# Solved 32x32 blocks of a delta rule: returned in four transfers to a compact tile, then placed by ScalarE and GpSimd

## What is computed

```
def _gated_delta_rule(q, k, v, beta, g):
    """S_t = exp(g_t) S_{t-1} (I - beta_t k_t k_t^T) + beta_t k_t v_t^T ; o_t = S_t^T q_t"""
    ...
    kb = k * beta[..., None]
    a_mat = jnp.where(strict, jnp.einsum("bhnid,bhnjd->bhnij", kb, k) * decay, 0.0)
    a_mat = a_mat + jnp.eye(c, dtype=q.dtype)
    rhs = jnp.concatenate([v * beta[..., None], kb * jnp.exp(g)[..., None]], axis=-1)
    sol = lax.linalg.triangular_solve(a_mat, rhs, left_side=True, lower=True,
                                      unit_diagonal=True)
    u, w = sol[..., :dv], sol[..., dv:]
    ...
    def step(state, inp):
        q_i, k_i, u_i, w_i, attn_i, gl_i = inp
        v_new = u_i - jnp.einsum("bhcd,bhde->bhce", w_i, state)
        ...
```

## Time and profile before

| | us |
|---|---|
| median of three runs | 3819.69 |
| lowest, highest | 3818.0, 3825.82 |
| span of the profiled execution | 3823.0 |
| TensorE busy in it | 3710.3 (97%) |
| VectorE busy | 2048.9 (54%) |
| ScalarE busy | 1089.4 (28%) |
| GpSimd busy | 69.4 (2%) |

### The profile page before, as it was taken

One profiled execution on the slowest core, in us unless ns is written; L12 is line 12 of the kernel. 1 busy time (PEld: TensorE's weight loads), 2 busy tenths in 40 slices (PEclk: granted clock), 3 DMA queues, 4 the chain that ended last, 5 costly groups with the idle time before them and its releaser, 6 DMA issues.

```text
span 3823.0 us, 43694 instructions
## 1 busy us (share of the span) xinstructions
PE 3710.3 (97%) x17964; PEld 3007.1 (79%) x17964; DVE 2048.9 (54%) x2527; ACT 1089.4 (28%) x1199; POOL 69.4 (2%) x80
## 2 busy tenths in 40 slices
PE   9999999989999999999999999999999998999998
PEld 8878888856778887888876678888888875778887
DVE  6564434563654445443766764434443766665443
ACT  3342222242432222222343222222222343322221
POOL 0000000000000000000110000000000102000000
PEclk9999999999999999999999999999999999999999
DMA  4212222110222222222412222222222413122221
GB/s 150 100 66 99 96 94 99 62 39 24 88 95 99 96 92 94 92 94 105 141 37 94 80 83 93 99 95 95 95 96 92 147 60 100 67 77 88 99 94 72
DMA packets 67766, 343.04 MB, mean 90 GB/s; under 512 B 23748, under 2 KB 23748, under 8 KB 32048
## 3 DMA queue, kind: packets, MB, share of 16 engines
q1 hardware_dynamic: 61872, 303.25, 22.4%
q0 software_dynamic: 5760, 37.86, 2.6%
HBM read 324.31 MB, written 16.78 MB: 89 GB/s over the span
## 4 chain that ended last, share of the span: by engine, by line
PE 88%; DVE 8%; ACT 2%; issue 1%; DMA 0%; SPq 0%; DVEq 0%; ACTq 0%
PE ACC L1003 26%; PE ACC L1004 25%; PE ACC L1005 25%; PE ACC L1669 1%; PE ACC L1497 1%; PE MIX L1497 1%; DVE WL L2340 1%; DVE PT L3172 0%; DVE PT L3170 0%; PE MIX L1724 0%; PE ACC L1411 0%; PE MIX L1462 0%; PE ACC L1010 0%; PE MIX L1423 0%; PE ACC L1657 0%
## 5 line engine op out<-in xcount | busy, mean ns | idle before, releaser
L1003 PE MATMUL ACC<-HH,WH 128*128 128x512 f32 (+1 forms) x3322 | 1305.6, 393 | 18.9 <-DVE X L2439 5.3
L1004 PE MATMUL ACC<-HL,WH 128*128 128x512 f32 (+1 forms) x3322 | 1290.4, 388 | 0.0
L1005 PE MATMUL ACC<-HH,WL 128*128 128x512 f32 (+1 forms) x3322 | 1290.4, 388 | 0.0
L2340 DVE TENSOR_TENSOR WL<-RAW,WH 128x2048 fp32r<-128x2048 f32 x291 | 667.4, 2293 | 445.7 <-ACT WH L1836 445.2
L1003 PEld LDWEIGHTS ACC<-HH,WH 128*128 128x128 f32 x3322 | 625.7, 188 | 165.0 <-issue 17.7
L1004 PEld LDWEIGHTS ACC<-HL,WH 128*128 128x128 f32 x3322 | 625.7, 188 | 130.3 <-issue 5.0
L1005 PEld LDWEIGHTS ACC<-HH,WL 128*128 128x128 f32 x3322 | 625.7, 188 | 128.5
L1836 ACT ACTIVATE WH<-RAW 128x2048 fp32r<-128x2048 f32 x291 | 554.7, 1907 | 599.3 <-PE ACC L1005 591.0
L2449 DVE TENSOR_TENSOR SG<-ACC,RS 128x512 f32<-128x512 f32 x132 | 91.3, 692 | 626.8 <-PE ACC L1005 626.6
L1005 PE MATMUL ACC<-HIDH,WL 128*128 128x512 f32 x1056 | 411.3, 389 | 0.0
L1004 PE MATMUL ACC<-HIDL,WH 128*128 128x512 f32 x1056 | 411.3, 389 | 0.0
(11 more groups left out here) (529 smaller groups left out, 2907.2 us busy)
## 6 DMA issues: line engine op xcount, KB each, us to landing
RAW<-wall SPq DMA_DIRECT2D x260, 1024.0 KB, 4.7
RAW<-wall SPq DMA_DIRECT2D x24, 768.0 KB, 4.1
KR<-spectra POOLq DMA_DIRECT2D x4, 2048.0 KB, 9.0
x_kept<-X POOLq DMA_DIRECT2D x2, 2048.0 KB, 6.8
FWK<-mats POOLq DMA_DIRECT2D x4, 1024.0 KB, 5.5
spectra<-SQ POOLq DMA_DIRECT2D x8, 512.0 KB, 3.0
spectra<-T POOLq DMA_DIRECT2D x8, 512.0 KB, 3.4
X<-x_kept POOLq DMA_DIRECT2D x2, 2048.0 KB, 14.5
```

Of the source, the lines that this page charges most:

```text
L1003: pe.matmul(out_ap, wh, hh, start=first, stop=False)
L1004: pe.matmul(out_ap, wh, hl, start=False, stop=False)
L1005: return pe.matmul(out_ap, wl, hh, start=False, stop=last)
L2340: v.tensor_tensor(WL[n % 2][:], RAW[n % 2][:], WH[n % 2][:], ALU.subtract).then_inc(w_lo, 1)
```

## The change

The two writes are cut by direction so that `blocks_out` is ordered by block row b first. Four reads, one per block row, bring everything into CB, a compact tile of 2 directions x 16 matrices x 32 columns on each of the 128 partitions. CB lies where BX lay, CT where the scratch BT lay. VectorE turns CB into CT, two transposes of 256 columns per pair. The first level reads CB and CT. ScalarE (`place_turned`) copies the blocks onto the diagonal of XIT, GpSimd onto that of XI, eight copies of 32 partitions x 256 columns each per pair; the second level waits for both. GpSimd zeroes all of XIT and, after the last spectrum is issued, XI[:, 1]. One semaphore now counts all four reads.

```diff
@@ sync
                     sp.wait_ge(blocks_solved, L + 1)
-                    sp.dma_start(blocks_out, BX[:]).then_inc(solved_sent, 16)
-                    sp.wait_ge(solved_sent, 16 * (L + 1))
-                    sp.wait_ge(dn_zero, 3 * L + 3)
-                    for p in range(2):
-                        for b in range(4):
-                            rows = slice(32 * b, 32 * b + 32)
-                            for d, dst in ((0, XI), (1, XIT)):
-                                src = blocks_out.rearrange("(d b p m) r x -> d b p r m x", d=2, b=4, p=2)[d, b, p]
-                                sp.dma_start(dst[rows, d, 8 * p:8 * p + 8, rows], src).then_inc(solved_landed[p], 16)
+                    for d in range(2):
+                        sp.dma_start(blocks_out.rearrange("(b d q) r x -> d b q (r x)", b=4, d=2)[d],
+                                     BX[64 * d:64 * d + 64].rearrange("p r x -> p (r x)")).then_inc(solved_sent, 16)
+                    sp.wait_ge(solved_sent, 32 * (L + 1))
+                    for b in range(4):
+                        src = blocks_out.rearrange("(b m) r x -> b r m x", b=4)[b]
+                        sp.dma_start(CB[32 * b:32 * b + 32].rearrange("p d m x -> p (d m) x"), src).then_inc(solved_landed, 16)
@@ gpsimd
                         if n == 4:
                             pool.wait_ge(kf_sp, 4 * l + 2)
-                            pool.memset(XIT[:, 1], 0.0).then_inc(dn_zero, 1)
+                            pool.memset(XIT[:], 0.0).then_inc(dn_laid, 1)
                         pool.wait_ge(kf_ev, 8 * l + n + 1)
                         pool.dma_start(spectra[o, :, fc, 2 * i:2 * i + 2], (SQ, T)[i][:]).then_inc(kf_out[i], 16)
+                    pool.wait_ge(kf_sp, 4 * l + 4)
+                    pool.memset(XI[:, 1], 0.0).then_inc(dn_laid, 1)
                     pool.wait_ge(kf_fd, 8 * l + 8)
                     for i in range(2):
                         pool.wait_ge(kf_out[i], 64 * (l + 1))
                     pool.dma_start(KR[0][:], spectra[0]).then_inc(kf_back[0], 16)
+                    pool.wait_ge(dn_laid, 6 * l + 4)
+                    for p in range(2):
+                        pool.wait_ge(dn_xt, 2 * l + p + 1)
+                        m = slice(8 * p, 8 * p + 8)
+                        for b in range(4):
+                            rows = slice(32 * b, 32 * b + 32)
+                            pool.tensor_copy(XI[rows, 0, m, rows], CB[rows, 0, m, :])
+                            k = pool.tensor_copy(XI[rows, 1, m, rows], CT[rows, 1, m, :])
+                        k.then_inc(dn_laid, 1)
@@ tensor, left
                     if lev == 0:
-                        pe.wait_ge(dn_xt, 4 * L + h + 1)
+                        pe.wait_ge(dn_xt, 2 * L + p + 1)
...
                         pe.wait_ge(dn_tc, 12 * L + 6 * p + a + 3)
+                        pe.wait_ge(solved_placed, 2 * L + p + 1)
+                        pe.wait_ge(dn_laid, 6 * L + p + 5)
                     for c in range(TC):
                         for d in range(2):
                             for near, far in joined(d, lev):
-                                mm = pe.matmul(ACC[far, 2 * a + d, columns(c, near)], DT[near, h, d, c, far], XI[near, d, TC * h + c, near],
-                                               start=True, stop=True)
+                                x = solved(d, 0)[near, d, TC * h + c, :] if lev == 0 else XI[near, d, TC * h + c, near]
+                                mm = pe.matmul(ACC[far, 2 * a + d, columns(c, near)], DT[near, h, d, c, far], x, start=True, stop=True)
@@ scalar
+                def place_turned(p):
+                    act.wait_ge(dn_xt, 2 * L + p + 1)
+                    act.wait_ge(dn_laid, 6 * L + 3)
+                    m = slice(8 * p, 8 * p + 8)
+                    for b in range(4):
+                        rows = slice(32 * b, 32 * b + 32)
+                        act.activation(XIT[rows, 0, m, rows], CT[rows, 0, m, :], ACT.Copy)
+                        k = act.activation(XIT[rows, 1, m, rows], CB[rows, 1, m, :], ACT.Copy)
+                    k.then_inc(solved_placed, 1)
...
                 copy_left(0, 0, 0)
                 copy_left(0, 1, 0)
+                place_turned(0)
                 grown_keys(0, 1)
...
                 copy_values(0, 1)
+                place_turned(1)
                 grown_keys(1, 0)
@@ vector
                 def turn_blocks(p):
-                    v.wait_ge(solved_landed[p], 128 * (L + 1))
+                    v.wait_ge(solved_landed, 64 * (L + 1))
                     v.wait_ge(kf_sp, 4 * L + 4)
-                    for h in (2 * p, 2 * p + 1):
-                        m = slice(TC * h, TC * h + TC)
-                        v.transpose(XIT[:, 0, m].rearrange("p c n -> p (c n)"), XI[:, 0, m].rearrange("p c n -> p (c n)"))
-                        v.transpose(XI[:, 1, m].rearrange("p c n -> p (c n)"), XIT[:, 1, m].rearrange("p c n -> p (c n)")).then_inc(dn_xt, 1)
+                    m = slice(8 * p, 8 * p + 8)
+                    for d in range(2):
+                        t = v.transpose(CT[:, d, m, :].rearrange("p c n -> p (c n)"), CB[:, d, m, :].rearrange("p c n -> p (c n)"))
+                    t.then_inc(dn_xt, 1)
```

More of the change, by code:

```diff
@@ L671, in build @@
         dn_at = sem("dn_at")
-        dn_zero = sem("dn_zero")
+        dn_laid = sem("dn_laid")
         blocks_sent = sem("blocks_sent")
@@ L676, in build @@
         solved_sent = sem("solved_sent")
-        solved_landed = [sem(f"solved_landed{i}") for i in range(2)]
+        solved_landed = sem("solved_landed")
+        solved_placed = sem("solved_placed")
         dn_xt = sem("dn_xt")
@@ L831, in build @@
         BX = put("BX", [P, 32, 32])
+        CB = place("CB", [P, 2, 4 * TC, 32], at=put.at[0] - 4 * 1024)
+        CT = place("CT", [P, 2, 4 * TC, 32], at=put.at[0])
         put = arena(put.at[0] + 4 * 1024)
@@ L950, in _ @@
                     pool.memset(BX[:], 0.0)
-                    pool.memset(XI[:, 0], 0.0).then_inc(dn_zero, 1)
-                    pool.wait_ge(dn_zero, 3 * l + 1)
-                    pool.memset(BX[:].rearrange("p r x -> p (r x)")[:, 0:1024:33], 1.0).then_inc(dn_zero, 1)
+                    pool.memset(XI[:, 0], 0.0).then_inc(dn_laid, 1)
+                    pool.wait_ge(dn_laid, 6 * l + 1)
+                    pool.memset(BX[:].rearrange("p r x -> p (r x)")[:, 0:1024:33], 1.0).then_inc(dn_laid, 1)
                     for h in range(4):
@@ L1361, in columns, with solved @@
                     return slice(c * P + rows.start, c * P + rows.stop)
+                def solved(d, turned):
+                    return CB if d == turned else CT
                 def left(p, a, lev):
@@ L1387, in right @@
                                 for near, far in joined(d, lev):
-                                    mm = pe.matmul(ACC[far, 2 * a + d, columns(c, near)], XIT[far, d, TC * h + c, far], YS[far, a, d, c, near],
+                                    xt = solved(d, 1)[far, d, TC * h + c, :] if lev == 0 else XIT[far, d, TC * h + c, far]
+                                    mm = pe.matmul(ACC[far, 2 * a + d, columns(c, near)], xt, YS[far, a, d, c, near],
                                                    start=True, stop=True)
@@ L1399, in right_turned @@
                             for near, far in joined(d, lev):
-                                mm = pe.matmul(ACC[near, 2 * a + d, columns(c, far)], YS[far, a, d, c, near], XIT[far, d, TC * h + c, far],
+                                xt = solved(d, 1)[far, d, TC * h + c, :] if lev == 0 else XIT[far, d, TC * h + c, far]
+                                mm = pe.matmul(ACC[near, 2 * a + d, columns(c, far)], YS[far, a, d, c, near], xt,
                                                start=True, stop=True)
@@ L2974, in solve_blocks @@
                     v.wait_ge(blocks_landed, 32 * (L + 1))
-                    v.wait_ge(dn_zero, 3 * L + 2)
+                    v.wait_ge(dn_laid, 6 * L + 2)
                     step(v.tensor_copy(BA[0:64], BG[0:64].rearrange("p r x -> p x r")))
@@ L3000, in keep_right @@
                     v.wait_ge(dn_t, 12 * L + 6 * p + a + 1)
+                    v.wait_ge(dn_laid, 6 * L + 4)
                     h = 2 * p + a
```

## The result

The changed kernel takes 3848.19 us (median of four runs, 3842.84 to 3850.55) against 3819.39 of the kernel before beside it: a ratio of 1.0068, 95% interval 1.0053 to 1.0082, or 28.8 us more. The forecast was slower, 3837, in a range of 3818 to 3842; the sign is right and the time lies above the range. All ratios here leave out executions far outside the others, of which there are two: one of `one_write` (10377 us) and one of the kernel before beside it (4403 us).

A forecast was written before the change was run, and what follows sets the result against it. TensorE was taken as the bound (88% of the chain), with the blocks' return hidden under its dummies. First levels late by 6.1 and 6.5 us plus 4.4 of clock made 17.0 on 3819.7, so 3837 us, range 3818 to 3842.

The forecast's parts named there:

- The return is hidden with 0.9 us to spare: Kernel before: the solved blocks' turns end at 2058.05, under the dummy matmuls, 0.9 us before the first level at 2058.95.
- Four shares for the write: Write of the solved blocks: its outermost loop of 4 spreads it over 4 engines, 32 packets each, 3.8 us more.
- The write lands at 2053.4: Write of the solved blocks, delayed by spectrum writes on the same engines: lands at 2053.4, between 2052.7 and 2054.5.
- The reads in 3.7 us: Four reads back of the solved blocks: 4096 packets pass in 3.7 us, after 0.9 us from issue to first packet.
- The change does not move that.: GpSimd's KR load: still issued at 2055.5, as the added memset ends 2 us before the wait for the spectra.
- Turns: VectorE's turns before the first level: four of 512 columns become two of 256, 0.75 us for both (0.6 to 1.4).
- The clock: TensorE after a 6 us pause: next dummies and small matmuls at the lower clock, 2.2 us per layer (0 to 4).
- What moved onto the other engines: Copies on ScalarE (0.39 us each) and GpSimd (0.3 to 1.0), turns on VectorE: nothing added, 4.4 us at ScalarE's far end.
- Hidden: Rival: the blocks' return stays hidden under the dummies by 2 us; 3819.5 us, range 3816 to 3824; chance 0.25.
- Copies: Rival: GpSimd copies over 1.1 us delay the second level; at 2 us, 8.7 us per layer, 3837; chance 0.05.
- One layer or a tail: Rival: reads caught by KR's load in one layer, or a short tail in both; +6 to +9 us, 3827; chance 0.10.
- faster: Rival: whole kernel faster by over 0.2%, needing 8 us, with no mechanism seen; chance 0.05.

The follow-up runs named there:

- one_write: The changed kernel with the write of the solved blocks as one transfer of 128 rows again and eight reads instead of four; 3821.73 us against 3822.97, ratio 0.9994.
- before_k20: The kernel before with 20 dummy matmuls instead of 28 ahead of the first level, all else as it was; 3820.55 us against 3822.85, ratio 0.9994.
- the three loops: Three kernels from `one_write`, with gaps in `blocks_out` making the write's DRAM side a loop of 8, 4 or 2; 3841.18, 3840.9 and 3850.26 us against 3822.29.
- kr_later: The changed kernel with the KR load held until the four reads have landed; 3834.21 us against 3822.97, ratio 1.0028.
- loop8: `one_write` with a gap in `blocks_out` after every 16 blocks, so the write is a loop of 8 over 16 rows; 3841.18 us against 3822.29, one execution.
- write_alone: The kernel before with only the two writes put in, its sixteen reads following the new block order; 3846.46 us against 3822.97, ratio 1.0059.
- eight_writes: The changed kernel with its write cut into eight transfers of 16 neighbouring rows, same layout and four reads; 3826.12 us against 3822.97, ratio 0.9997.
- reads_first_k14: `one_write` with 14 dummies instead of 28 and the last two spectrum writes held until the reads have landed; 3817.46 us against 3823.74, ratio 0.9987.
- loop4: `one_write` with a gap in `blocks_out` after every 32 blocks, so the write is a loop of 4 over 32 rows; 3840.9 us against 3822.29, one execution.
- loop2: `one_write` with one gap in the middle of `blocks_out`, so the write is a loop of 2 over 64 rows; 3850.26 us against 3822.29, one execution.

## Why the prediction was right or wrong

**The return is hidden with 0.9 us to spare.** Right in what matters, and loose in a detail. With the write undone the level starts at the end of the dummies. But the level of the first head waits for the first two turns only, and those end at 2056.87 (the second starts at 2056.20 and takes 0.67), so it had 2.1 us; `before_k20` shows it, where that level starts 6.3 us after the first dummy. Nothing in the sum hung on it.

**Four shares for the write.** Right, as far as the count of packets in flight tells. It was argued from form; the three loops (6.9, 3.4 and 1.65 in flight for 8, 4 and 2) and the 4.0 of the changed kernel now show it. Which engines carry them the trace doesn't tell.

**The write lands at 2053.4.** Wrong, and this is the step where the forecast first failed: it landed 4.0 us later, at 2057.4. I priced 32 packets on an engine at the 0.16 us of a packet in the kernel before and added 0.7 us for the spectra. The write of the changed kernel in two stretches, SP's queue over 2047.4 to 2051.4, and then both queues over 2051.4 to 2057.0:

```profile
q1 hardware_dynamic: 51, 0.20, 24.9%
```

```profile
q0 software_dynamic: 267, 0.98, 50.9%
q1 hardware_dynamic: 84, 0.32, 14.5%
```

In the first 4.0 us four packets are in flight throughout (24.9% of 16 is 4.0), but only 51 pass, where 100 at 0.16 us would have fitted: 0.249 x 64 us / 51 = 0.31 us for each. So when the spectra come, 84 packets are left in place of some 30. These are at 0.155 us again (0.145 x 89.6 / 84), but only 2.3 are in flight, with 8.1 of the spectra's beside them (50.9% of 16). The slow packets cost 49 x 0.16 / 4 = 2.0 us. The sharing cost 5.6 - 84 x 0.16 / 4 = 2.2 us, of which I had 0.7. Together they are 3.5 of the 4.0 us, and 0.4 is the later start of the stage (the first issue at 2045.72 in place of 2045.36). The range for this term, to 2054.5, had no room for either: the duration of a packet was taken as a constant of its size.

**The reads in 3.7 us.** Not tested as such in the changed kernel, since the last one is caught. In `kr_later` they land 4.5 us after their first issue, where 0.9 + 3.7 were predicted. Three of the four reads of the changed kernel landed by 2061.1; only the last waited until 2067.99.

**"The change does not move that."** Wrong for KR's issue, and this is the term of the sum that failed: the level waits for the load's end, and the load came 3.9 us late. I looked at what GpSimd does ahead of it, and the added memset indeed ended 5.6 us before the wait did. But that wait is for the spectra, and the slow write was still under way beside them: the last two took 7.1 and 7.3 us from issue to landing in place of 3.2 and 3.8, and the load was issued at 2059.38, 3.9 us later than before. They were slow at their start as well as at their end. GpSimd's queue in a stretch of 1 us, the kernel before over 2051.5 to 2052.5 and the changed one over 2051.9 to 2052.9, each 1.3 us after the issue of the first of the two:

```profile
q0 software_dynamic: 97, 0.40, 96.4%
```

```profile
q0 software_dynamic: 5, 0.02, 16.8%
```

I had allowed 0.5 us for the engines' backlog, and at the wrong place. The catch itself was right: the last read lands with the load, at 2067.99 and 2067.88, the load 8.5 us after its issue (8.3 predicted). So the release is late by 3.7 us (2067.99 against 2064.3), nearly all of it because the load is. `loop8` shows the same catch with the load on time: late by 6.5 and 6.0 us, where 6.1 and 6.5 were predicted.

**Turns.** 0.77 us for two, 0.75 predicted. The level is late by 9.5 and 9.0 us where the sum had 6.1 and 6.5: 5.9 us too little over both layers.

**The clock.** The sign and the place were right, the size was too large. From the level to the keys the changed kernel takes 13.1 and 14.0 us where it took 12.0 and 12.5, so 2.7 us over both layers where I had 4.4. In the first layer's chain the ten dummies cost 1.3 us more and not 2.1 (3.75 for 2.43), and the level's small matmuls 0.4 and not 0.1. The 0.105 us that the forecast adds to a pass is near what the trace of the kernel before has: the dummies' passes start 0.213 us apart from 2052.24 to 2054.80, at a grant of 0.50, and 0.111 us apart from 2055.17 to 2058.74, at 1.00. But the grant was 0.50 only until 2072.66, and the ten dummies, from 2069.92, ran 3.75 us. Another 2.8 us stand in the convolution of layer 1. Its windows, the kernel before and then the changed one:

```profile
2149.44:2213.25 63.81, 55.57 (x245) 42.84 (x246) 52.15 (x43) 7.71 (x8) 0.00 (x0) 0.95 0.14 50
```

```profile
2160.33:2226.98 66.65, 58.42 (x245) 44.75 (x246) 52.12 (x43) 7.71 (x8) 0.00 (x0) 0.90 0.13 48
```

The same 245 instructions take 2.8 us more at a grant of 0.90 in place of 0.95. These can't be put down to the change. `one_write`, which loses nothing, has the same 0.90 in its second layer, and `write_alone`, which has nearly the whole loss, has 0.95 in both. The second layer of `one_write`, then the first of `write_alone`:

```profile
3327.67:3394.33 66.66, 58.42 (x245) 44.80 (x246) 52.14 (x43) 7.71 (x8) 0.00 (x0) 0.90 0.13 48
```

```profile
2156.38:2220.21 63.83, 55.59 (x245) 42.79 (x246) 52.14 (x43) 7.71 (x8) 0.00 (x0) 0.95 0.13 50
```

So what is left for the clock, in this trace, are the 2.7 us behind the two levels. They are a balance: 3.3 us more up to the second level, and 0.6 less from there to the keys, where VectorE has fewer columns to turn.

**What moved onto the other engines.** Right. The timeline of the changed kernel:

```profile
2068.92 0.39 POOL L980 COPY XI<-CB 32x256 f32<-32x256 f32 x1 [9.01 <-DVE CT L3024]
2071.38 0.40 ACT L2150 ACTIVATE XIT<-CT 32x256 f32<-32x256 f32 x1
```

A copy on ScalarE takes 0.40 us (0.39 predicted), one on GpSimd 0.39, near the low end of my 0.3 to 1.0. GpSimd's eight are done 3.2 us after the level's start, and the second level begins 9.0 us after it, held by VectorE's XIT and not by a copy:

```profile
2077.81 0.68 PE L1395 MATMUL ACC<-XI,DT 64*64 64x64 f32 x16 [0.76 <-DVE XIT L3028]
```

**The rivals.** "Hidden" is false as a forecast of this kernel; the mechanism it names is the one of `one_write` and `eight_writes`, where it holds. Its premise, a write that isn't held to four packets in flight, is what separates them (11.0 in `eight_writes`, 4.0 in the changed kernel): `eight_writes` takes 3826.1 us with it, and the changed kernel, with the same layout and reads, 3848.2 without it. "Copies" is false here; `reads_first_k14` has its wait, for another reason than price. "One layer or a tail" and "faster" have nothing for them.

**The sum.** 17.0 us became 24.4 in the trace: 18.5 for 12.6 at the levels, 2.7 for 4.4 by the clock, 2.8 in a convolution that no run ties to the change, and 0.4 before the stage. Of the miss, 5.9 us are the late release, and the clock's term, too large by 1.7, hid part of it; that part is luck. The medians differ by 28.8, as the profiled execution of the kernel before, at 3825.8, was the slowest of its four. The prediction laid a difference of spans on the median 3819.7; the width of the runs, 8 us, should have been in the range.

## What to carry to other kernels

When a layout change gives one side of a transfer a short outermost loop, count that loop before the bytes: here 4 instead of 128 made a 0.5 MB write of 1.4 us one of 9.5, and cutting it into more transfers or keeping it whole put it right at no cost that could be measured (ratios 0.9997 and 0.9994). Price the whole neighbourhood of such a transfer: the spectra under way beside it took 7.1 and 7.3 us in place of 3.2 and 3.8, and KR's load, which waits for them, moved by 3.9, so "the change doesn't touch that instruction" is no proof that its time stands. A path shortened under cover showed nothing here until the cover was cut (`one_write` 0.9994, and 0.9976 with 20 dummies), and the cover is only as long as the clock makes it: 20 dummies took 4.7 us at a grant of 1.00 and 6.4 at 0.73. A new reader of the result should not stand behind an unrelated wait in its engine's queue, as in `reads_first_k14`, where the second level waited 5.1 us for it.

## What the runs showed of the hardware

The duration of a packet was not a constant of its size. A 4 KB packet of the write from BX took 0.159 us in the kernel before (all 128 in the first layer, 126 in the second), but a mean of 0.31 in the first four microseconds of the changed kernel (up to 0.8), and 0.31 in `eight_writes`, where 97 of 128 took over 0.2 us in the first layer. It is not bound to few packets in flight, as `eight_writes` had eleven. `one_write`, with one whole transfer, has 0.159 throughout. `loop8`, `loop4` and `loop2` begin slow in the first layer (means of 0.31 to 0.35 in the first microsecond) and are back at 0.159 later, `loop8` and `loop2` from the fourth microsecond on, `loop4` from the seventh. No run here tells what makes them slow.

Larger transfers were slow beside the write with four packets in flight: the spectra's 512 KB writes went from 3.2 and 3.8 us to 7.1 and 7.3, and in `write_alone` they took 7.1 and 7.4. They moved 5 packets in a stretch where 97 passed before, and in their last microsecond, 2057.0 to 2058.0, some two were in flight. What slows this end no run here tells; the trace doesn't tell the engines apart.
